# Sums of squares on another engine in the opening, paired first blocks in the short down stages, and head norms one block sooner, in a fused streaming encoder step

## The chip, the cores and the metric

One core of one Trainium2 chip runs the whole program. The engines are TensorE (PE; its weight loads are PEld), VectorE (DVE), ScalarE (ACT), GpSimd (POOL) and SyncE (SP), which issues the weight loads from HBM. The metric is the device time of one execution in microseconds. Before: a median of 2714.54 us over 3 runs, 2713.57 to 2715.55.

## The reference, cut

Two groups of requests (512 prompt tokens, 8 samples of 16 tokens, so 640 token columns) go through two layers of width 1024:

```python
def run_trunk(x, p, ...):
    for i in range(DEPTH):                                   # 2 layers
        x = x + 0.5 * swiglu(rmsnorm(x, norm_g[i, 0]), ffn_w_gu[i, 0], ffn_w_d[i, 0])
        xn = rmsnorm(x, norm_g[i, 1])
        y, st = even_mixer(xn, ...) if i % 2 == 0 else odd_mixer(xn, ...)
        x = x + y
        x = x + 0.5 * swiglu(rmsnorm(x, norm_g[i, 2]), ffn_w_gu[i, 1], ffn_w_d[i, 1])
        xg = rmsnorm(x, norm_g[i, 3])
        x = x + (p[i] @ w_ple[i]) * jax.nn.sigmoid(xg @ w_ple_gate[i])
    y = rmsnorm(x, final_norm)

def even_mixer(xn, ...):
    qkv_a, z_a, beta_a, a_a, q_b, k_b, v_b, o_b, i_b, f_b = split(xn @ w_in)
    qkv_a = silu(causal_dwconv(hist, gdn_conv_w))
    q_a = l2norm(q_a.reshape(B, T, H_A, DK_A)) * (DK_A ** -0.5)   # the head norms: 4 of q, 4 of k
    k_a = l2norm(k_a.reshape(B, T, H_A, DK_A))
    ...  # gated delta rule and mLSTM, chunked; output projection
```

The hidden width of each SwiGLU is 2816. All is computed in float32.

## The kernel before, in words

Activations lie transposed: `x` is 128 partitions by 8 blocks (KD) by 640 tokens. Every weight block (a 128-column strip, `kt` k steps of 128 rows) is split into a high part `whi` (ScalarE's cast, `prep`, L1595 to L1607) and a low part `wlo` (POOL's subtraction, L861, or DVE's in places), and every activation likewise (`xh`/`xl`, `hh`/`hl`). A product `mm` (L898 to L919) makes, in each k step, six matmuls of 128x320: high by high, high by low and low by high for both halves of the tokens. Results go to one of four PSUM slots; semaphore `job_done` tells of a finished block, `slot_free` of a free slot. The high and low parts of a block lie in a ring of three pairs of slots (`place_run` gives the order), so a cast waits until the block that had its slots is done. The order of work on each engine is written out by hand, stage by stage; each engine goes through its own list in order.

The opening (`kind == "load"`): PE transposes the eight blocks of x (L982) and, between them, makes the k steps of the first two weight blocks as the low parts `xl` come (`x_low`, L2269). ScalarE copies x (L1787), makes `xh` (L1650), and after its loop casts the third block (`prep(2)`) and squares the blocks of x (L1813). DVE copies the rest of x, makes `xl`, the tau sums (L2228 to L2231, `tau_sums`, inputs of the FFN's fast products), the copies of the states, and then adds the squares up (`square_sum`, L2278 and L2280). Behind the third block PE multiplies the sum by a matrix of ones (`norm_job`, L968), ScalarE takes the root (L1732), DVE the reciprocal (L2366). POOL makes the low parts from the third block on. `plain_start` is DVE's order in the first FFN stage.

Each FFN is done in three parts of 8, 8 and 6 hidden blocks (PARTS): a "gu" stage that makes them and a "down" stage that multiplies them by `kt` = 8, 8 or 6 k steps into the eight blocks of x. Block 0 of a down stage waits in each k step for the hidden block (`h_ready`, from `hidden_low`, L2793); with `kt` = 6 it is the last part (`last`), and for every finished block DVE scales it (L2181), updates x (L2919), adds the square that ScalarE makes (L1659, L2280) and makes the new low part (L2269), while ScalarE makes the high part (L1650) and casts the weight block after the next but one. In the second FFN of a layer (`"pT" in s`), PE transposes the layer's embedding behind block 1 and DVE copies it (L2941, L2943). The next stage's first block takes the x blocks k step by k step (`xg_ready`) and is followed by its norm product.

The even mixer's stage `even_in` has 12 convolved blocks (NA), a block of gates, and 12 plain blocks. DVE also makes the rows of the gates (`row_steps`, in the first five plain blocks). The head norms are tied to the plain blocks: from block HN_LAG = 4 on, ScalarE squares one head (L1739), PE sums it (L968), ScalarE takes the root (L1747, one tile `root`, so it waits for DVE's use of the root before), DVE the reciprocal and the scaling (`head_norm`, L2373, L2374). Then `core` starts: PE drains the slots, spreads rows (L1051), fills with blocks of z and waits for DVE's scaled keys (L2398) at L1057.

## Time and profile before

| what | us |
|---|---|
| median of 3 runs | 2714.54 |
| profiled execution, its own time | 2713.01 |
| its span, first to last instruction | 2711.3 |
| PE busy | 2652.8 |
| PEld busy | 2613.9 |
| DVE busy | 1863.9 |
| ACT busy | 1075.4 |
| POOL busy | 524.6 |

The mean granted clock of TensorE is 0.991 of full speed; it is below 1 in the opening, at some places between 866 and 959 us (the end of the mixer's core) and at the very end. A matmul's duration in a row (about 0.31 us) is not its cost: they are pipelined, and starts are about 0.147 us apart. "Idle before" in square brackets is the time in which the engine had nothing, and behind the arrow stands what released it.

### The profile page before, as it was taken

How to read it: one execution, taken by the hardware profiler on the slowest of the kernel's cores; microseconds unless marked ns; L12 is line 12 of the kernel's file. 1: busy time of each engine (PE TensorE's matmuls, PEld its weight loads, DVE VectorE, ACT ScalarE, POOL GpSimd, SP SyncE). 2: the span in 40 equal slices, each digit the busy share in tenths (PEclk: the TensorE clock that was granted, in tenths of full speed). 3: DMA queues.
4: the chain of work that ended last, by engine and by line, in shares of the span. 5: the costliest groups of instructions: out<-in, count | busy, mean ns of one | idle time of the engine just before them, and what ended most of it. 6: DMA issues, size and time to landing. Idle time of an engine off the chain costs nothing.

```text
span 2711.3 us, 43605 instructions
## 1 busy us (share of the span) xinstructions
PE 2652.8 (98%) x18155; PEld 2613.9 (96%) x18155; DVE 1863.9 (69%) x2188; ACT 1075.4 (40%) x1565; POOL 524.6 (19%) x249
## 2 busy tenths in 40 slices
PE   7999999999999999999999999999999999999998
PEld 7999999999998799999999999999999999999998
DVE  7748386988667768576577874847666786584756
ACT  5525254233222645344244552524411254252545
POOL 1030303232010030201113302030333311102041
PEclk9999999999999999999999999999999999999999
DMA  4323223232003122323232232232222223232231
GB/s 122 86 71 89 83 75 90 55 81 55 17 9 86 54 72 78 94 78 94 63 88 70 71 101 71 78 94 75 83 78 79 63 78 94 63 95 65 82 101 50
DMA packets 401180, 205.57 MB, mean 76 GB/s; under 512 B 15586, under 2 KB 398971, under 8 KB 400984
## 3 DMA queue, kind: packets, MB, share of 16 engines
q1 hardware_dynamic: 400778, 202.70, 26.4%
q8 instruction: 144, 2.36, 0.4%
q14 instruction: 52, 0.43, 0.1%
q10 hardware_dynamic: 206, 0.08, 0.0%
HBM read 195.14 MB, written 7.60 MB: 75 GB/s over the span
## 4 chain that ended last, share of the span: by engine, by line
PE 54%; DVE 9%; ACT 2%; issue 1%; POOL 0%; DVEq 0%; ACTq 0%
PE ps L928 9%; PE ps L930 9%; PE ps L929 9%; PE ps L913 9%; PE ps L917 8%; PE ps L914 8%; DVE ut L2181 1%; DVE x L2919 1%; DVE sumsq L2280 1%; DVE r L2366 1%; DVE hf L2787 1%; DVE x L3105 0%; DVE wlo L2197 0%; DVE hl L2269 0%; PE ps L1198 0%
## 5 line engine op out<-in xcount | busy, mean ns | idle before, releaser
L861 POOL TENSOR_TENSOR wlo<-raw,whi 128x1024 fp32r<-128x1024 f32 (+2 forms) x212 | 513.1, 2423 | 2147.0 <-ACT whi L1607 2146.6
L913 PE MATMUL ps<-xh,whi 128*128 128x320 f32 x1520 | 464.0, 313 | 12.1 <-POOL wlo L861 4.7
L914 PE MATMUL ps<-xl,whi 128*128 128x320 f32 x1520 | 458.4, 309 | 0.0
L913 PE MATMUL ps<-hh,whi 128*128 128x320 f32 x1440 | 437.6, 312 | 5.1 <-DVE hl L2793 2.9
L914 PE MATMUL ps<-hl,whi 128*128 128x320 f32 x1440 | 434.8, 310 | 0.0
L928 PE MATMUL ps<-tau_hi,whi 128*128 128x320 f32 x1296 | 401.3, 310 | 2.1 <-DVE wlo L2197 2.0
L929 PE MATMUL ps<-tau_lo,whi 128*128 128x320 f32 x1296 | 400.5, 309 | 0.0
L930 PE MATMUL ps<-tau_hi,wlo 128*128 128x320 f32 x1296 | 400.5, 309 | 0.0
L1607 ACT CAST whi<-raw 128x1024 fp32r<-128x1024 f32 (+2 forms) x214 | 206.7, 967 | 395.0 <-PE ps L917 355.6
L917 PE MATMUL ps<-xh,wlo 128*128 128x320 f32 x1520 | 347.1, 310 | 0.0
L917 PE MATMUL ps<-hh,wlo 128*128 128x320 f32 x1440 | 329.1, 310 | 0.0
L2181 DVE TENSOR_TENSOR ut<-ps,r 128x640 f32<-128x640 f32 x112 | 92.4, 825 | 328.0 <-PE ps L917 327.0
L913 PEld LDWEIGHTS ps<-xh,whi 128*128 128x128 f32 x1520 | 286.3, 188 | 18.5 <-issue 11.0
L914 PEld LDWEIGHTS ps<-xl,whi 128*128 128x128 f32 x1520 | 286.3, 188 | 0.9 <-issue 0.2
L1618 ACT CAST whi<-raw 128x512 fp32r<-128x512 f32 (+1 forms) x243 | 185.0, 766 | 246.9 <-PE ps L930 125.6
L913 PEld LDWEIGHTS ps<-hh,whi 128*128 128x128 f32 x1440 | 271.4, 189 | 8.1 <-DVE hl L2793 4.5
L914 PEld LDWEIGHTS ps<-hl,whi 128*128 128x128 f32 x1440 | 271.3, 188 | 0.4
L917 PEld LDWEIGHTS ps<-xh,wlo 128*128 128x128 f32 x1520 | 254.7, 188 | 0.0
L928 PEld LDWEIGHTS ps<-tau_hi,whi 128*128 128x128 f32 x1296 | 243.2, 188 | 4.5 <-issue 3.9
L929 PEld LDWEIGHTS ps<-tau_lo,whi 128*128 128x128 f32 x1296 | 243.3, 188 | 0.0
L930 PEld LDWEIGHTS ps<-tau_hi,wlo 128*128 128x128 f32 x1296 | 243.3, 188 | 0.0
L917 PEld LDWEIGHTS ps<-hh,wlo 128*128 128x128 f32 x1440 | 241.4, 188 | 0.0
(433 smaller groups left out, 4829.4 us busy)
## 6 DMA issues: line engine op xcount, KB each, us to landing
raw<-in_ffn_w_gu SPq DMA_DIRECT2D x324, 256.0 KB, 3.9
raw<-in_ffn_w_d SPq DMA_DIRECT2D x64, 512.0 KB, 4.0
raw<-in_w_in_even SPq DMA_DIRECT2D x32, 512.0 KB, 4.1
raw<-in_ffn_w_d SPq DMA_DIRECT2D x32, 384.0 KB, 3.6
raw<-in_w_in_odd SPq DMA_DIRECT2D x24, 512.0 KB, 3.7
raw<-in_w_ple_gate SPq DMA_DIRECT2D x16, 512.0 KB, 3.9
raw<-in_ffn_w_gu SPq DMA_DIRECT2D x14, 512.0 KB, 4.6
raw<-in_w_out_even SPq DMA_DIRECT2D x8, 512.0 KB, 4.0
```

The costliest lines, as they stand in the source:

```text
L861: pool.tensor_tensor(ring(wlo, n), raw[:, slot, 0:kt, :], ring(whi, n).bitcast(fp32), ALU.subtract).then_inc(lo_ready, 1)
L913: pe.matmul(ps[j % 4][:, c, 0:HT], wh[:, k], hi[:, k, cs], start=(k == 0), stop=False)
L914: pe.matmul(ps[j % 4][:, c, 0:HT], wh[:, k], lo[:, k, cs], start=False, stop=False)
L917: last = pe.matmul(ps[j % 4][:, c, 0:HT], wl[:, k], hi[:, k, cs], start=False, stop=(k == kt - 1))
L928: pe.matmul(out, whi[:, w], hi(i), start=(start and i == 0), stop=False, skip_group_check=True)
L929: pe.matmul(out, whi[:, w], lo(i), start=False, stop=False, skip_group_check=True)
L930: last = pe.matmul(out, wlo[:, w], hi(i), start=False, stop=(i == KH - 1), skip_group_check=True)
L1607: act.copy(ring(whi, n), raw[:, raw_pos["block", n], 0:kt, :]).then_inc(hi_ready, 1)
L1618: act.copy(group_ring(whi, g), group_raw(p, g)).then_inc(pair_hi, 1)
L2181: o1(dve.tensor_tensor(out, a, b, ALU.mult))
L2280: own(dve.tensor_tensor(sumsq[:], sumsq[:], src, ALU.add).then_inc(sm, 1), sm)
L2366: o1(dve.reciprocal(r[:], r[:]))
```

## The change

Three edits. (1) In the opening ScalarE's squares move into its loop over x, two blocks behind the high parts, the cast of the third weight block moves from behind the loop to its step 5, and the first two blocks' results are copied out after the squares. The additions of the squares go from DVE to POOL: `add_square(1)` to `add_square(3)`, then the third block's low part, then `add_square(4)` to `add_square(7)`. In `plain_start` the order of three steps changes. (2) In down stages with fewer than 8 k steps PE makes all steps but the last of blocks 0 and 1, then the last step of both. (3) HN_LAG goes from 4 to 3, so that the eight head norms go with plain blocks 3 to 10 in place of 4 to 11.

```diff
--- before.py
+++ after.py
@@ -457,7 +457,7 @@
         gcol0 = 4 * HA * P
         bcol = [gcol0 + 2 * HA + q * HB * P for q in range(4)]
         icol = bcol[3] + HB * P
-        HN_LAG = NA - 2 * HA
+        HN_LAG = NA - 2 * HA - 1
         s = dict(kind="even_in", n0=len(blocks), prod=prod - 1, pos=[], l2=[], side=side(prod - 1))
         for q in range(3):
             for h in range(HA):
@@ -472,7 +472,7 @@
                 blk((w_in, bcol[q] + h * P), KD, "plain")
                 s["pos"].append([8, 12, 20][q] + h)
 
-                if q * HB + h >= HN_LAG:
+                if HN_LAG <= q * HB + h < HN_LAG + 2 * HA:
                     s["l2"].append(job("hn"))
         stages.append(s)
         Z_ORDER = [0, 1, 2, 4, 3, 5, 6, 7]
@@ -861,9 +861,21 @@
                 pool.tensor_tensor(ring(wlo, n), raw[:, slot, 0:kt, :], ring(whi, n).bitcast(fp32),
                                    ALU.subtract).then_inc(lo_ready, 1)
 
-            n = 2
+            def add_square(q):
+
+                pool.wait_ge(sq_ready, q + 1)
+                a, b = ([qcopy, stt] if q == 1 else [sumsq, [qcopy, stt][q % 2]])
+                step(pool.tensor_tensor(sumsq[:], a[:], b[:], ALU.add))
+                pool.sem_inc(sq_added, 2 if q == 1 else 1)
 
             pool.wait_ge(lo_ready, 2)
+            for q in range(1, 4):
+                add_square(q)
+            low(2, KD)
+            for q in range(4, KD):
+                add_square(q)
+            pool.sem_inc(sumsq_done, 1)
+            n = 3
             while n < NB:
                 kt = blocks[n][1]
                 if n == 12:
@@ -1516,8 +1528,15 @@
                 elif kind == "down":
                     if s.get("split"):
                         first_blocks(s)
+                    hidden = (h_ready, s["hbase"])
+                    both = s["kt"] < KD
+                    if both:
+                        for part in ((0, s["kt"] - 1), (s["kt"] - 1, s["kt"])):
+                            for o in range(2):
+                                mm(s["n0"] + o, *s["hid"], first=hidden, part=part)
                     for o in range(2 if s.get("split") else 0, KD):
-                        mm(s["n0"] + o, *s["hid"], first=(h_ready, s["hbase"]) if o == 0 else None)
+                        if not both or o > 1:
+                            mm(s["n0"] + o, *s["hid"], first=hidden if o == 0 else None)
                         if o == 1 and "pT" in s:
 
                             pe.wait_ge(p_loaded, 32 * (s["layer"] + 1))
@@ -1536,7 +1555,7 @@
                         tposes(j, [((b - first) // 4, b % 4 * P, cacoll[:, b, :]) for b in range(first, last)])
                     for b in range(NA):
                         mm(n + NA + 1 + b, *s["side"])
-                        if b >= HN_LAG:
+                        if HN_LAG <= b < HN_LAG + 2 * HA:
                             q = b - HN_LAG
 
                             pe.wait_ge(hn_sq, s["hn0"] + q + 1)
@@ -1781,6 +1800,12 @@
                     act.dma_start(vstage[a:b, 1, :], ins["conv_c_w"][0].rearrange("j (k p) -> (j k) p", p=P)).then_inc(in_loaded[1], 16)
                     act.dma_start(vstage[b:b + HB, 1, :], ins["mlstm_norm_w"][0].rearrange("(k p) -> k p", p=P)).then_inc(in_loaded[1], 16)
                     act.dma_start(vstage[b + HB:b + HB + 1, 1, :], ins["gdn_norm_w"]).then_inc(in_loaded[1], 16)
+                    def square(q):
+                        if q >= 2:
+
+                            act.wait_ge(sq_added, q - 1)
+                        act.activation([qcopy, stt][q % 2][:], x[:, q, :], ACT.Square).then_inc(sq_ready, 1)
+
                     for q, j in enumerate(s["x"]):
 
                         act.wait_ge(job_done, done_at(j))
@@ -1798,7 +1823,10 @@
                         x_high(0, q, 0)
                         if q == 0:
                             prep(1)
-                    prep(2)
+                        if q >= 2:
+                            square(q - 2)
+                        if q == 5:
+                            prep(2)
 
                     def first_out(n, out):
                         j = block_job[n]
@@ -1806,16 +1834,11 @@
                         act.wait_ge(job_done, done_at(j))
                         act.copy(halves(out[:]), ps[j % 4][:, :, 0:HT]).then_inc(slot_free[j % 4], 1)
 
-                    for q in range(KD):
-                        if q >= 2:
-
-                            act.wait_ge(sq_added, q - 1)
-                        act.activation([qcopy, stt][q % 2][:], x[:, q, :], ACT.Square).then_inc(sq_ready, 1)
-                        if q == 3:
-                            first_out(0, gt)
-                            prep(3)
-                        if q == 5:
-                            first_out(1, ut)
+                    square(KD - 2)
+                    square(KD - 1)
+                    first_out(0, gt)
+                    prep(3)
+                    first_out(1, ut)
                 elif kind == "gu":
                     p0, count, n0 = s["p0"], s["count"], s["n0"]
 
@@ -1957,14 +1980,15 @@
                         own(act.activation(c, a, ACT.Relu, bias=bias, scale=sgn).then_inc(row_act, 1), row_act)
                     for b in range(NA):
                         q = b - HN_LAG
-                        if q >= 0:
+                        heads_due = 0 <= q < 2 * HA
+                        if heads_due:
                             if q == 0:
 
                                 act.wait_ge(conv_out, NA)
                             head_squares(s, q, s["l2"], qkv[:, q, :])
                         if b >= 2:
                             prep_next(n + NA + 1 + b, 2)
-                        if q >= 0:
+                        if heads_due:
                             head_root(s, q, s["l2"][q], 1.0)
                 elif kind == "core":
                     z0 = s["z0"]
@@ -2755,9 +2779,6 @@
                     o1(dve.tensor_copy(ccstate[:].rearrange("p a b -> p (a b)"), ps[j % 4][:, 1, 0:KD * DECB * CC]))
                     o1(dve.tensor_copy(vec2[:], ps[j % 4][:, 1, KD * DECB * CC:KD * DECB * CC + NV2]))
                     free(j)
-                    for q in range(KD):
-                        square_sum(0, q)
-                        dve.sem_inc(sq_added, 1)
                 elif kind == "gu":
                     p0, count = s["p0"], s["count"]
 
@@ -2831,12 +2852,12 @@
                     def plain_start():
                         t = s["tau"]
                         tau_rest(t, 0)
-                        tau_rest(t, 1)
                         norm_recip(s)
                         copied_gate()
-                        tau_sums_alone(3)
+                        tau_rest(t, 1)
                         copied_hidden()
                         plain_gate(1)
+                        tau_sums_alone(3)
                         tau_rest(t, 2)
                         hidden_low(0)
                         if s["plain"] > 3:
@@ -3065,7 +3086,7 @@
                         if b < len(row_steps):
                             row_steps[b]()
                         q = b - HN_LAG
-                        if q >= 0:
+                        if 0 <= q < 2 * HA:
                             head_norm(s, q, qkv[:, q, :], float(DK) ** -0.5 if q < HA else 1.0)
                 elif kind == "core":
```

## Rows read from the trace of the kernel before

**Rows 1.** The page, busy time (share of the span) and instructions of each engine.

```profile
PE 2652.8 (98%) x18155; PEld 2613.9 (96%) x18155; DVE 1863.9 (69%) x2188; ACT 1075.4 (40%) x1565; POOL 524.6 (19%) x249
```

**Rows 2.** PE's waits over the span: engine line <- releaser: total us, times, longest.

```profile
PE ps L968 <- DVE sumsq L2280: 5.1, 2, 4.9
...
PE ps L913 <- DVE hl L2793: 2.9, 6, 0.8
```

**Rows 3.** PE in order of time, opening: start, us, what, idle before <- releaser.

```profile
28.81 0.41 PE L913 MATMUL ps<-xh,whi 128*128 128x320 f32 x1 [0.67 <-DVE xl L2269]
...
34.03 0.31 PE L913 MATMUL ps<-xh,whi 128*128 128x320 f32 x1
...
46.09 2.50 PE L968 MATMUL ps<-sumsq,one 128*128 128x320 f32 x4 [4.87 <-DVE sumsq L2280]
```

**Rows 4.** Windows: PE, PEld, DVE, ACT, POOL busy (x), granted clock, DMA share, GB/s.

```profile
41.00:51.00 10.00, 5.13 (x17) 4.12 (x16) 8.19 (x7) 8.18 (x10) 4.18 (x2) 0.66 0.38 107
```

**Rows 5.** DVE in order of time, opening.

```profile
27.88 0.88 DVE L2269 SCALAR_TENSOR_TENSOR xl<-x,vec,xh 128x640 fp32r<-128x640 f32 x1
...
30.14 2.61 DVE L2228 SCALAR_TENSOR_TENSOR tau_row<-x,vec,xg_back 128x320 f32<-128x320 f32 x1
...
45.22 0.83 DVE L2280 TENSOR_TENSOR sumsq<-sumsq,stt 128x640 f32<-128x640 f32 x1
```

**Rows 6.** POOL in order of time, opening and first short down stage.

```profile
30.02 2.37 POOL L861 TENSOR_TENSOR wlo<-raw,whi 128x1024 fp32r<-128x1024 f32 x1 [25.35 <-ACT whi L1607]
...
424.65 1.84 POOL L861 TENSOR_TENSOR wlo<-raw,whi 128x768 fp32r<-128x768 f32 x1 [5.46 <-ACT whi L1607]
...
437.10 2.03 POOL L861 TENSOR_TENSOR wlo<-raw,whi 128x768 fp32r<-128x768 f32 x1 [2.98 <-ACT whi L1607]
442.11 2.04 POOL L861 TENSOR_TENSOR wlo<-raw,whi 128x768 fp32r<-128x768 f32 x1 [2.98 <-ACT whi L1607]
```

**Rows 7.** PE and DVE in order of time, layer 0, first FFN's last down stage.

```profile
424.82 0.42 PE L913 MATMUL ps<-hh,whi 128*128 128x320 f32 x1 [0.84 <-DVE hl L2793]
...
469.81 1.24 PE L968 MATMUL ps<-sumsq,one 128*128 128x320 f32 x4
...
426.08 0.82 DVE L2181 TENSOR_TENSOR ut<-ps,r 128x640 f32<-128x640 f32 x1 [1.31 <-PE ps L917]
...
443.43 1.39 DVE L2919 SCALAR_TENSOR_TENSOR x<-ut,x 128x640 f32<-128x640 f32 x1
...
467.80 0.89 DVE L2269 SCALAR_TENSOR_TENSOR xl<-x,vec,xh 128x640 fp32r<-128x640 f32 x1
```

**Rows 8.** ScalarE, DVE and PE in order of time, layer 0, second FFN.

```profile
1410.42 0.84 ACT L1607 CAST whi<-raw 128x768 fp32r<-128x768 f32 x1 [2.22 <-PE ps L917]
...
1410.43 0.82 DVE L2181 TENSOR_TENSOR ut<-ps,r 128x640 f32<-128x640 f32 x1 [1.31 <-PE ps L917]
1421.41 0.69 DVE L2941 CAST hh<-ps 128x512 fp32r<-128x512 f32 x1
...
1452.82 0.38 PE L913 MATMUL ps<-xh,whi 128*128 128x320 f32 x1 [0.32 <-issue]
```

**Rows 9.** PE and DVE in order of time, layer 1, second FFN.

```profile
2581.14 0.41 PE L913 MATMUL ps<-xh,whi 128*128 128x320 f32 x1 [1.52 <-DVE xl L2793]
...
2626.35 0.39 PE L913 MATMUL ps<-xh,whi 128*128 128x320 f32 x1 [0.73 <-POOL wlo L861]
...
2587.67 0.82 DVE L2181 TENSOR_TENSOR ut<-ps,r 128x640 f32<-128x640 f32 x1 [0.99 <-PE ps L917]
```

**Rows 10.** ScalarE, DVE and PE in order of time, head norms and the core's start.

```profile
609.69 0.80 ACT L1747 ACTIVATE root<-ps,eps 128x640 f32<-128x640 f32 x1 [9.24 <-DVE qkv L2374]
...
604.59 4.15 DVE L2373 RECIPROCAL inv<-root 128x640 f32<-128x640 f32 x1
...
612.79 1.24 PE L968 MATMUL ps<-sq,one 128*128 128x320 f32 x4
...
655.64 0.57 PE L1051 MATMUL ps<-R,ident 128*128 128x128 f32 x3 [1.09 <-issue]
...
662.98 1.16 PE L1057 MATMUL ps<-W,qkv 128*128 128x128 f32 x8 [1.70 <-DVE W L2398]
```

## The prediction

> **What bounds the kernel now.** The first look goes to the busy table: TensorE (PE) is busy for 98% of the span [rows 1]. So only time in which PE stands still, or runs at the lower clock, can be won; some 58 us in all. The second look is the list of PE's waits: the longest one by a compute engine is the single wait of 4.9 us for the opening's sum of squares; the one on the hidden blocks comes six times and adds up to 2.9 us [rows 2]. The third look, PE's order of time, places them. In the opening PE's third block begins at 34.03 and would go straight into the norm product, but this starts at 46.09 after 4.87 idle [rows 3]; the granted clock from 41 to 51 us is 0.66, so part of that stretch ran at 1.2 GHz in place of 2.4 [rows 4]. That block gives the unit for all below: eight k steps (six matmuls each) from 34.03 to 41.2, 0.88 us a step with the last one's drain.
>
> **The opening.** Removed: eight operations of DVE, the last of which ends at 46.05 [rows 5]. Added: seven additions of 128x640 on GpSimd (POOL), from about 19 us on, interleaved with DVE's own work, and the third block's low part between them. No row has such an addition. The nearest are POOL's subtractions: 1.84 us for 768 columns, 2.37 for 1024 [rows 6], so 2.07 ns a column and 1.58 us for 640. Upper bound 1.84; below 1.3 nothing speaks for. Seven are 11 us.
>
> What they lie beside decides. At 30.02 POOL starts its only subtraction of this stretch; DVE's 128x320 operation issued at 30.14 takes 2.61 us and ends 0.36 after POOL's, where the like are near 0.55 [rows 5, 6]. So a DVE operation with two SBUF inputs stands still while POOL reads SBUF, and here nearly all of DVE's are such. At 442.11 the reverse is seen: POOL takes 2.04 in place of 1.84 since DVE was in first [rows 6]. They take turns.
> The Trainium skill, SBUF — State Buffer, "SBUF: two separate sides", states the same as a rule: the pair of ports is an exclusive lock held for a whole instruction. By this rule the move from DVE to POOL buys no overlap in the opening; without it the opening would gain 6.5 us (rival A). The trace agrees with the rule in the operation at 30.14.
>
> Walking the order: addition 1 (19.1 to 20.7) holds up the low part of x block 3, PE loses 0.3. Addition 2 falls into the tau sums, so that x block 4's low part ends 2.3 us late, at 26.0. Addition 3, the third block's low part and addition 4 (1.6 + 2.4 + 1.6) all fall on the next four tau sums, which stand ahead of x block 6 on DVE. PE starts that step at 28.81 now, right behind DVE's operation of 27.88, after a wait of 0.67 [rows 3, 5]: no cover. It moves to about 35.5, with 5.4 us of idle PE before it. x block 7 and everything behind are ready (last addition near 42). From 35.5 PE has two steps, the state transposes (1.4) and the third block: 1.8 + 1.4 + 1.8 + 7.2 = 12.2, so the norm product starts at 47.7, against 46.09, and wants no wait. The new stall draws the lower clock as the old one did, which costs 0.8 to 2.5 after it; but the norm product (2.50 us now [rows 3], 1.24 at the full clock [rows 7]) and the block behind it lose the 2.6 us that they pay today. Net: +1.6 + 1.6 - 2.6 = **+0.6 us**. Bounds: -6.5 (no blocking) and +4 (POOL's operations keep the ports back to back). The new order behind it (tau low part 1 later, the last tau sums later) moves DVE by about 1 us under blocks that keep PE busy for 21 us: nothing.
>
> **The down stages with six k steps (four: layer 0 and 1, each FFN).** Now PE does five steps, waits for the sixth hidden block (0.84, 0.84, 0.84 and 1.52 idle), finishes block 0 and goes on. The change puts five steps of block 1 (4.4 us) into the wait. Face value: the whole loss, 1.0 + 1.0 + 1.0 + 1.7 = -4.7 us. What this moves: block 0 is finished after eleven steps in place of six and the wait: in the first case from 426.0 to 429.4, +3.4. Behind it hangs DVE's chain of each block (scale, update x, ScalarE's square, sum, low part), on which ScalarE's next cast and POOL's next low part hang too. Its period is 5.01 us [rows 6] (its last two starts), PE's is six steps, 5.28. So a late start is won back by 0.27 a block at most, and the last two periods of a stage are longer than PE's (bigger weights, next stage).
> First case: DVE starts block 0 at 426.08 and makes the last x low part from 467.80 on; PE needs it at its own 468.8 and starts the norm product at 469.81 [rows 7]. No cover. After: block 0's chain begins at 429.5, block 1's is not held up by the idle gap of today, and its update ends at 436.2 against 434.8; +1.4 stays to the end, the norm product starts **+1.3**. The third case (layer 1, first FFN) has the same ring order: **+1.3**.
> Second case (layer 0, second FFN): the weight ring gives block 2 the slots of block 0. ScalarE casts block 2 at 1410.42, the moment that block 0 is done, and DVE begins at 1410.43 [rows 8]. Both move by the whole 3.4. Here DVE also copies two transposed blocks (4.3 us), so its chain runs without idle to the end of the stage, and PE's gate block of the next stage waits for it (0.32 idle at 1452.82 [rows 8], a cast behind that chain): **+3.4**.
> Fourth case: block 0 is done 2.7 later (the stall is longer today), the chain's idle wait for block 1, which starts at 2587.67 [rows 9], takes some back; the rest reaches the small blocks that PE waits for at 2626.35 [rows 9]: **+2.3**.
> Sum **+8.3 us**; bounds -4.7 (face value) and +13.6 (3.4 in each). I take the sum since in each case a row shows PE at zero slack on that chain.
>
> **Head norms a block sooner.** Gain: after the last block no norm follows. PE waits 1.09 before 655.64 and 1.70 before 662.98 [rows 10], the latter for a product that stands behind a reciprocal and a scaling of DVE (5.0 us). Without these it is ready by 660.2 and PE, from 655.4 on 5.4 us of work, is there at 660.9: -2.1. Cost: the four first norms move into DVE's and ScalarE's crowded time. The root of head 1 waits 9.24 us for DVE's head 0, whose reciprocal starts at 604.59 [rows 10], behind the row steps. Now head 2's sum at 612.79 just finds its square; with the shift the fourth sum stands there (613.5), whose square waits for root 2, which waits for DVE's head 1: 609.2 + 5.0 = 614.3, then root and square 1.7: 616.0. PE stalls 2.4 (0.8 if POOL misses DVE's row steps). Net **+0.3**, bounds -2.1 and +0.8.
>
> **Sum.** 0.6 + 8.3 + 0.3 = +9.2 on the profiled execution's 2713.0 gives 2722.2; the median shown is 1.5 above that execution: 2723.8. Five new stalls of 2 to 5 us lie between ones that left the clock (1.70) and one that took it down (4.87); one more episode at 1.2 GHz, priced by half the lost 2.6, is 0.7 on average where DVE's pace doesn't hide it: **2724.5 us**.
>
> **Rivals.** A: POOL and DVE work side by side in the opening. For it: both only read most of those tiles. Against: the 2.61. Opening -6.5, in all +2.1: 2716.6. Chance 0.13.
> B, the other side: DVE's later start is absorbed and the down stages give their face value. It decides by whether the last x low part is later than PE's seventh step into the next stage; today's distance is 0.1 us. With opening +0.6 and heads -1: -5.1, 2709.4; with A as well -13, 2701. Together 0.12.
> C: the new stalls bring the lower clock several times, unhidden: +15 to +18, 2729.5 to 2732.5. Chance 0.13.
> D: the reordered blocks don't change PE's waits at all, since DVE's chain hides it: within 2 of 2714.5. Chance 0.04. The forecast, 2718 to 2729: 0.58.
>
> Range 2712 to 2730. 0.2% is 5.4 us, about what a measurement of this kernel can tell from none. Faster than 2709.1: 0.09. Slower than 2720: 0.69 (forecast 0.55, C 0.13, a little of A). Same: 0.22.
>
> **What would show it.** Right: DVE operations of 2 us and more between 19 and 42 us, and PE idle over 4 us ahead of x block 6; no wait before the opening's norm product; PE waiting for an x low part just ahead of the norm product behind both first FFNs; in the second FFNs PE waiting 2 to 3 us for POOL at down block 5; a wait of 2.4 for a head's square near 614. Wrong: PE entering the third block before 36 us; the norm product of the even mixer starting earlier relative to its down stage than now; 2716 or less.

## The result and the profile after

| kernel | median us | lowest to highest | runs | ratio to before (95%) |
|---|---|---|---|---|
| before, beside it | 2714.06 | 2709.13 to 2721.57 | 6 | |
| after | 2732.4 | 2724.65 to 2734.18 | 6 | 1.0065 (1.0051 to 1.0079) |

Slower by 0.65%, 2.4 us above the range (2712 to 2730). The ratios here and below are not the quotients of the medians and differ from them by up to 0.1%. One execution of the kernel before, of those beside e5 to e8, took 3698.81 us at a mean clock of 0.651 and is left out of the ratios. The profiled execution took 2734.18 us, its span 2732.4 at a mean granted clock of 0.986 (before: 2711.3 at 0.991). The executions of the changed kernel fall into two groups of spans, near 2723 and near 2731; the profiled one is of the upper. Where the gap of 8 us between them is made is asked below. The kernel before has groups too: of its 88 other executions on record 23 have spans of 2705.6 to 2707.8, 3 of 2709.3 to 2709.9, 59 of 2711.2 to 2714.2 and 3 of 2719.8 to 2720.9; the trace of before is of the third.

The busy table of after, to set against [rows 1]. DVE's eight additions are gone (2188 to 2180 instructions), POOL has seven more, and PE, whose work is the same, is busy for 15.5 us more, though it has the same 18155 matmuls: the first sign that the granted clock is part of the answer.

```profile
PE 2668.3 (98%) x18155; PEld 2627.5 (96%) x18155; DVE 1866.6 (68%) x2180; ACT 1074.1 (39%) x1565; POOL 535.4 (20%) x256
```

PE's waits of after, in the form of [rows 2]. The wait of 4.9 for the sum of squares is gone from the list. In its place stand the low part of x (`xl`) in the opening, POOL's low parts (`wlo`) in the down stages and the head's square (`ut`).

```profile
PE ps L925 <- POOL wlo L861: 11.0, 15, 2.7
PE ps L925 <- DVE xl L2293: 9.1, 4, 3.5
...
PE ps L980 <- ACT ut L1758: 2.3, 1, 2.3
...
PE ps L925 <- DVE hl L2293: 1.6, 1, 1.6
```

POOL in order of time in the opening of after (L868 is the addition, L861 the third block's low part):

```profile
19.29 1.58 POOL L868 TENSOR_TENSOR sumsq<-qcopy,stt 128x640 f32<-128x640 f32 x1 [14.63 <-ACT stt L1807]
...
27.06 2.10 POOL L868 TENSOR_TENSOR sumsq<-sumsq,stt 128x640 f32<-128x640 f32 x1 [3.49 <-ACT stt L1807]
29.34 2.42 POOL L861 TENSOR_TENSOR wlo<-raw,whi 128x1024 fp32r<-128x1024 f32 x1 [0.18 <-POOL sumsq L868]
31.73 1.78 POOL L868 TENSOR_TENSOR sumsq<-sumsq,qcopy 128x640 f32<-128x640 f32 x1
```

DVE beside it. The tau sums take 0.55 where POOL is idle and 1.7 to 2.6 where it is not; each ends 0.3 to 0.4 after the POOL operation beside it.

```profile
27.79 1.73 DVE L2252 SCALAR_TENSOR_TENSOR tau_row<-x,vec,xg_back 128x320 f32<-128x320 f32 x1
29.55 2.57 DVE L2253 SCALAR_TENSOR_TENSOR tau_row<-x,vec,xg_back 128x320 f32<-128x320 f32 x1
32.16 1.70 DVE L2254 SCALAR_TENSOR_TENSOR tau_row<-x,vneg,tau_row 128x320 f32<-128x320 f32 x1
33.89 0.55 DVE L2255 SCALAR_TENSOR_TENSOR tau_row<-x,vneg,tau_row 128x320 f32<-128x320 f32 x1
```

And PE in order of time, with every new wait of the three edits and the norm product of the opening, which waits for nothing, to set against [rows 3], [rows 7] to [rows 10]:

```profile
26.27 0.48 PE L925 MATMUL ps<-xh,whi 128*128 128x320 f32 x1 [2.09 <-DVE xl L2293]
...
35.61 0.41 PE L925 MATMUL ps<-xh,whi 128*128 128x320 f32 x1 [3.47 <-DVE xl L2293]
...
50.80 0.70 PE L980 MATMUL ps<-sumsq,one 128*128 128x320 f32 x2
...
472.41 0.41 PE L925 MATMUL ps<-xh,whi 128*128 128x320 f32 x1 [1.53 <-DVE xl L2293]
...
619.91 0.54 PE L980 MATMUL ps<-ut,one 128*128 128x320 f32 x1 [2.35 <-ACT ut L1758]
...
663.52 0.68 PE L1063 MATMUL ps<-R,ident 128*128 128x128 f32 x4 [1.21 <-issue]
...
1430.73 0.38 PE L925 MATMUL ps<-hh,whi 128*128 128x320 f32 x1 [0.99 <-POOL wlo L861]
1449.47 0.39 PE L925 MATMUL ps<-hh,whi 128*128 128x320 f32 x1 [2.67 <-POOL wlo L861]
...
1983.17 0.41 PE L925 MATMUL ps<-hh,whi 128*128 128x320 f32 x1 [1.55 <-DVE hl L2293]
...
2624.39 0.61 PE L925 MATMUL ps<-xh,whi 128*128 128x320 f32 x1 [2.64 <-POOL wlo L861]
2647.88 0.39 PE L925 MATMUL ps<-xh,whi 128*128 128x320 f32 x1 [0.77 <-POOL wlo L861]
```

The traces are compared by landmarks that PE passes once: the norm products (their start), the core's first matmul, the core's last transpose; and one of DVE, the last hidden block's low part in the first FFN. Each entry is the difference of that landmark's time to the first trace of before, less the same at the landmark ahead of it. In brackets stands the time at the lower clock in that stage. "Whole" is the changed kernel; the second to fourth column of it are further executions of the same program (e4, e13, e14), and e11 is the kernel before once more.

| stage, up to | before | after | whole, e4 | whole, e13 | whole, e14 | before, e11 |
|---|---|---|---|---|---|---|
| norm product of the opening | 46.09 (5.6) | +4.7 (10.2) | +5.5 (17.1) | +1.7 (6.8) | +4.9 (13.7) | +1.4 (1.2) |
| last hidden block of FFN 1 | 423.94 (4.7) | -2.1 (0) | -2.1 (0) | -2.1 (0) | -2.1 (0) | +0.5 (5.6) |
| norm of even mixer | 469.81 (0) | +1.0 (0) | +1.0 (0) | +1.0 (0) | +1.0 (0) | 0 (0) |
| core's start | 655.64 (0) | +4.3 (3.4) | +4.3 (3.4) | +4.2 (3.4) | +2.7 (0) | 0 (0) |
| core's end | 959.72 (30.7) | +6.4 (47.8) | -1.6 (30.7) | -0.1 (34.1) | -1.8 (30.7) | +8.4 (47.8) |
| norm behind FFN 2, layer 0 | 1459.93 (0) | +4.2 (3.4) | +3.0 (0) | +4.2 (3.4) | +3.0 (0) | -0.1 (0) |
| norm of odd mixer | 1964.73 (0) | +0.9 (0) | +0.9 (0) | +0.9 (0) | +0.9 (0) | 0 (0) |
| norm behind FFN 2, layer 1 | 2643.48 (0) | +2.1 (3.4) | +2.1 (0) | +2.1 (3.4) | +2.1 (0) | 0 (0) |
| end | 2711.28 (8.4) | -0.4 (6.0) | 0 (7.3) | -0.3 (6.1) | 0 (7.2) | -0.4 (5.4) |
| sum | | +21.2 | +13.1 | +11.5 | +10.5 | +9.7 |

Two things are read from it. What the edits do comes again from execution to execution, but for the opening (+1.7 to +5.5) and for 1.2 to 1.6 us in two stages where 3.4 us at the lower clock come or stay away: +10.5 to +13.1 in all where the core runs about as in the first trace. And the largest single entry of after, +6.4 in the core, is one that the unchanged kernel has too, in e11.

### The profile page after: what moved, and what is told of

Read it like the earlier page. It is cut to its first block, busy times and chain, and to the rows that moved or that the text cites. A ratio compares the mean times of both kernels' runs of the same rounds, so it can differ in the third digit from the quotient of the medians.

```text
span 2732.4 us, 43606 instructions
## 1 busy us (share of the span) xinstructions
PE 2668.3 (98%) x18155; PEld 2627.5 (96%) x18155; DVE 1866.6 (68%) x2180; ACT 1074.1 (39%) x1565; POOL 535.4 (20%) x256
## 3 DMA queue, kind: packets, MB, share of 16 engines
q1 hardware_dynamic: 400778, 202.70, 26.2%
## 4 chain that ended last, share of the span: by engine, by line
PE 79%; DVE 16%; ACT 2%; issue 2%; POOL 0%; DMA 0%; DVEq 0%; SPq 0%; ACTq 0%
PE ps L940 12%; PE ps L941 12%; PE ps L942 12%; PE ps L925 11%; PE ps L929 11%; PE ps L926 11%; PE ps L1069 3%; DVE x L2940 2%; PE ps L1095 2%; DVE ut L2205 1%; DVE sumsq L2304 1%; DVE ct L2995 1%; PE ps L1063 1%; DVE ct L2992 1%; DVE r L2390 1%
## 5 line engine op out<-in xcount | busy, mean ns | idle before, releaser
L861 POOL TENSOR_TENSOR wlo<-raw,whi 128x1024 fp32r<-128x1024 f32 (+2 forms) x212 | 511.6, 2416 | 2135.8 <-ACT whi L1626 2135.4
L925 PEld LDWEIGHTS ps<-hh,whi 128*128 128x128 f32 x1440 | 271.5, 189 | 11.5 <-issue 5.9
```

Source lines behind the costliest of these rows:

```text
L861: pool.tensor_tensor(ring(wlo, n), raw[:, slot, 0:kt, :], ring(whi, n).bitcast(fp32), ALU.subtract).then_inc(lo_ready, 1)
L925: pe.matmul(ps[j % 4][:, c, 0:HT], wh[:, k], hi[:, k, cs], start=(k == 0), stop=False)
```

## The experiments

**One edit alone (e1 to e3), and all three again (e4).** The theory was three separate mechanisms: the shared ports in the opening, DVE's chain in the short down stages, the row steps ahead of the head norms. The rival for each was that its part does nothing or gains.

e1, the opening alone (cut and put in fewer lines; the new order in `plain_start` is in it too):

```diff
@@ POOL
+            for q in range(1, 4): add_square(q)
+            low(2, KD)
+            for q in range(4, KD): add_square(q)
@@ ScalarE, loop over x
+                        if q >= 2: square(q - 2)
+                        if q == 5: prep(2)
@@ DVE
-                    for q in range(KD): square_sum(0, q) ...
```

> The opening's edit alone. The theory (GpSimd's additions and VectorE's work take turns on SBUF, so the x block steps of TensorE are held up ahead of a stall of some 3.5 us): the norm product of the opening starts near 50.8 us as in the changed kernel, every later stage is shifted by 2.5 us and no more, time +2.5 us against the kernel before. Rival (the reordered start of the first FFN or the clock behind it costs on its own): a shift that grows behind 60 us. Rival that the core's lower clock belongs to this edit: +10 us.

Measured: 2716.72 us (11 runs) beside 2713.49, ratio 1.0013 (1.0005 to 1.0022), so +3.2 us; its trace is of its fastest execution (2713.78) and shows +0.8. PE waits 5.00 ahead of x block 6, and the norm product comes at 48.72, where 50.8 was expected: +2.6, with 2.1 of it given back behind it:

```profile
35.00 0.64 PE L925 MATMUL ps<-xh,whi 128*128 128x320 f32 x1 [5.00 <-DVE xl L2285]
```

e2, the down stages alone:

```diff
+                    both = s["kt"] < KD
+                        for part in ((0, s["kt"] - 1), (s["kt"] - 1, s["kt"])):
+                            for o in range(2): mm(s["n0"] + o, *s["hid"], first=hidden, part=part)
```

> The paired first blocks alone, in the four down stages with six k steps. The theory (TensorE has no slack on VectorE's chain, which starts 3.4 us later): +1.0, +4, +1.0 and +2.5 us at the four stages, +8.5 us in all. Rival (the later start of VectorE's chain is absorbed, face value): -4.7 us. The waits for the sixth hidden block, 0.84 us thrice and 1.52 once, are gone in either case.

Measured: 2720.9 us (6 runs), ratio 1.0033 (1.0021 to 1.0045), so +7.4 us. By stages, counted from the last hidden block: +1.2, +4.3 (with 3.4 us at the lower clock), +1.1, +2.1.

e3, the head norms alone (the guards that end the eight heads at block 10 are cut here):

```diff
-        HN_LAG = NA - 2 * HA
+        HN_LAG = NA - 2 * HA - 1
```

> The head norms one block sooner, alone. The theory: TensorE waits 2.4 us for the square of the fourth head near 614 us, which also brings 3.4 us at the lower clock (1.7 lost), and gains 2.1 at the core's start: +2.0 us up to the core. Rival (the lower clock that cost 8 us in the core of the changed kernel comes with this edit, which makes the core start on another footing): +10 us in most runs. Without that: +2 us.

Measured: 2716.95 us (11 runs), ratio 1.0011 (1.0001 to 1.002), so +3.5 us, over executions that fall apart: spans of 2709.0 to 2709.3 (4 of 11), one of 2712.7 (the trace) and 2715.1 to 2717.5 (6 of 11). The wait came, and behind it 3.4 us at the lower clock: the stage ahead of the core is 4.2 us longer. In the core the gain stands in every trace of this edit: from the core's first matmul to the product at L1057 PE takes 5.49 us in place of 7.34, and from 10 to 140 us into the core it is 2.0 us ahead of before (in the whole change 1.7 from there on).

```profile
617.64 1.34 PE L968 MATMUL ps<-ut,one 128*128 128x320 f32 x4 [2.35 <-ACT ut L1739]
```

e4, the whole change:

> The changed kernel itself once more, beside the three parts and on the same chip. If the 8 us in the core are a matter of how the stretches at the lower clock fall in a run, the runs fall into two groups near 2723 and 2732 us, and runs of the kernel before show such groups too; if they belong to the change, all runs of the kernel before stay below 2716 and nearly all of this one lie near 2732.

Measured: 2728.67 us (6 runs), ratio 1.0062 (1.005 to 1.0075), so +15.2 us against 3.2 + 7.4 + 3.5 = 14.1 for the parts. The parts add up within 1.1, though that is in part luck, since the three slowest of the six executions of e4 belong to the upper group and the median lies between the groups. Stage by stage each edit's cost is found again in the whole. The opening and the down stages lose by their medians (3.2 and 7.4) as by their stages (0.5 in e1's fastest execution, and 8.7); of the heads the stages show a loss of 0.7 or 2.2 us, and the median's 3.5 holds more of the clock in the core than of the edit.

**How much of block 1 goes into the wait (e5).** If the later end of block 0 is what costs, one step of block 1 (0.88 us, as long as the wait) fills the wait and leaves block 0 where it was.

```diff
+                        last_ = s["kt"] - 1
+                        for o, part in ((0, (0, last_)), (1, (0, 1)), (0, (last_, s["kt"])), (1, (1, s["kt"]))):
+                            mm(s["n0"] + o, *s["hid"], first=hidden, part=part)
```

> Against the kernel before, in the four short down stages only one k step of block 1 (0.88 us) goes into TensorE's wait, so block 0 is finished when it is now. The theory (the stage ends by VectorE's chain, which begins with block 0): the wait's 3.5 us are worth nothing at stages one to three (0 to -0.2 us each) and at most 0.8 at the fourth, where the wait is longest; in all -1 us. Rival (TensorE itself is the bound, the paired kernel lost by something else): nearly the whole of the wait, -3.5 to -4.5 us.

Measured: 2716.66 us (11 runs), ratio 1.0009 (1.0 to 1.0018). The three waits of 0.84 are gone, and the fourth is 0.65 in place of 1.52:

```profile
2588.49 0.42 PE L913 MATMUL ps<-xh,whi 128*128 128x320 f32 x1 [0.65 <-DVE xl L2800]
```

The four down terms fall from +1.2, +4.3, +1.1, +2.1 to -0.9, -0.1, -0.9 and -0.4. So the loss was the later end of block 0. The expectation held in the sum's direction and missed in the first FFNs: there 0.9 of 1.0 is won where 0 to 0.2 was expected, so DVE's chain follows PE in these stages and doesn't bound them by itself. In the second case 0.1 of 1.0 reaches the norm product, as expected of a chain that is the bound. In the fourth, 0.87 less of the first wait is set against a wait for POOL that grows from 0.73 to 1.19. The sum is -2.2, for -1 expected; the median is 3.2 above before's. The trace puts this down to the core (+7.7, 47.8 us at the lower clock); 6 of the 11 executions, the profiled one among them, lie in an upper group of spans (2714.9 to 2718.1, the others 2710.3 to 2711.2), and that the five others of it have the same long core is not shown.

**The row steps later (e6).** If the heads' wait comes from row steps that stand ahead of head 1's reciprocal on DVE, two of them two blocks later take it away and leave the gain.

```diff
+                    ROW_AT = [0, 1, 2, 4, 6]
-                        if b < len(row_steps):
-                            row_steps[b]()
+                        if b in ROW_AT:
+                            row_steps[ROW_AT.index(b)]()
```

> Head norms one block sooner as in the change, but the last two row steps of VectorE (maxima, keys) wait for blocks 4 and 6 in place of 3 and 4, so that the first head norms stand ahead of them. The theory (the 2.4 us wait near 614 comes from VectorE's row steps ahead of head 1): no wait for a head's square, no stretch at the lower clock before the core, TensorE 2.1 us earlier at the core's first product than in the kernel before; 5 to 6 us faster than the heads' edit alone. Rival (the single tile of the roots is the cause whatever stands ahead): the wait stays, +3.5 us.

Measured: 2708.69 us (11 runs), ratio 0.9988 (0.998 to 0.9997). PE has no wait at a norm product from 600 us to 650, and DVE's two reciprocals stand 6.0 us apart:

```profile
603.93 4.15 DVE L2374 RECIPROCAL inv<-root 128x640 f32<-128x640 f32 x1
...
609.95 4.15 DVE L2374 RECIPROCAL inv<-root 128x640 f32<-128x640 f32 x1
```

In after the row steps lie between them (11.2 us from 601.93 to 613.11). With e3 it shows both sides of the third edit: a gain of 2.0, and a wait of 2.35 that is not part of it. Of the 4.4 us that the trace of e6 wins, 3.6 lie in the core; the 1.6 of them above the edit's 2.0 go with the clock there, 27.3 us at the lower one against 30.7.

**The additions taken away or halved (e7, e8).** The opening's edit again, with POOL's additions for q > 1 left out (e7) or over half of the columns (e8). The semaphores, the order and ScalarE's squares stay. In both the sum of squares lacks columns or blocks, so what is computed behind it is not the reference's.

```diff
@@ e7
-                step(pool.tensor_tensor(sumsq[:], a[:], b[:], ALU.add))
+                if q == 1:
+                    step(pool.tensor_tensor(sumsq[:], a[:], b[:], ALU.add))
@@ e8
-                step(pool.tensor_tensor(sumsq[:], a[:], b[:], ALU.add))
+                z = slice(0, T if q == 1 else HT)
+                step(pool.tensor_tensor(sumsq[:, z], a[:, z], b[:, z], ALU.add))
```

> The opening's edit with six of the seven additions on GpSimd left out (the sum of squares holds two blocks only, so the first norm is wrong); orders, waits and semaphores stay. The theory (GpSimd's additions hold VectorE's operations up): without them only the third block's low part holds VectorE, TensorE's waits of 2.1 and 3.5 us shrink to under 1 us together, the norm product starts near 42.5 us and the time is 5 to 7 us below the opening's edit. Rival (the waits come from ScalarE's new order, squares and cast in its loop): waits and norm product within 1 us of the opening's edit.

> The opening's edit with the six later additions on GpSimd over 320 columns in place of 640 (the rest of the sum is left out). GpSimd's 1.58 us become 0.9. The theory: each VectorE operation that an addition holds up ends 0.7 us sooner, so the step of x block 4 starts 0.7 and that of x block 6 some 2 us sooner than with the opening's edit (26.3 and 35.6 us), the norm product about 2 us sooner besides what the clock adds. Rival (ScalarE's order): no change at either step.

Measured: 2711.53 us (10 runs), 0.9993 (0.9984 to 1.0003), and 2712.81 us (10 runs), 0.9999 (0.999 to 1.0008). The wait ahead of x block 6 is 5.00 with the additions whole (e1), 3.66 with halves and 2.70 without. DVE's same tau sum (the third of x blocks 4 and 5) in e1, e8 and e7:

```profile
31.54 1.70 DVE L2246 SCALAR_TENSOR_TENSOR tau_row<-x,vneg,tau_row 128x320 f32<-128x320 f32 x1
```

```profile
30.57 1.03 DVE L2247 SCALAR_TENSOR_TENSOR tau_row<-x,vneg,tau_row 128x320 f32<-128x320 f32 x1
```

```profile
28.39 0.55 DVE L2247 SCALAR_TENSOR_TENSOR tau_row<-x,vneg,tau_row 128x320 f32<-128x320 f32 x1
```

The duration of DVE's operation follows that of POOL's (1.77, 1.11, none). The step of x block 6 starts at 33.35 with halves (33.6 expected) and at 30.70 without. The 2.70 that stay are not the additions': POOL's low part falls into the same tau sums, since ScalarE's cast of the third block was put into its loop. The rows of e7:

```profile
25.40 2.61 POOL L861 TENSOR_TENSOR wlo<-raw,whi 128x1024 fp32r<-128x1024 f32 x1 [5.94 <-ACT whi L1620]
...
25.77 2.58 DVE L2246 SCALAR_TENSOR_TENSOR tau_row<-x,vec,xg_back 128x320 f32<-128x320 f32 x1
```

So 2.3 of the 5.0 us are the additions, and of the rest the row of 2.58, where the like take 0.55, accounts for 2.0. That it is there because of the earlier cast is read from the rows; no run takes the cast alone back. The expectation for e7 fell short here: the waits at x blocks 4 and 6 were to shrink under 1 us together and are 0.90 and 2.70, and the norm product starts at 45.88, not near 42.5. Part of that is what the rival named, ScalarE's new order.

**An opening without POOL's additions (e9).** If the ports are the trouble and the norm's wait of 4.9 is DVE's additions coming late, the additions must stay on DVE, but start early: squares 0 to 3 in ScalarE's loop, first addition behind x low part 1, and the fourth block's low part behind them on DVE.

```diff
@@ ScalarE, loop over x
+                        if q == 2:
+                            square(0); square(1)
+                        if q in (3, 4):
+                            square(q - 1)
@@ DVE
+                        if q == 1:
+                            add_square(1)
...
+                    for q in range(2, KD):
+                        add_square(q)
+                    dve.wait_ge(lo_ready, 3)
+                    low(3)
```

> Another opening on the kernel before: the additions stay on VectorE, but the first lies in its idle time near 16 us, ScalarE squares blocks 2 and 3 in its loop and does its copies and the cast of the fourth weight block ahead of the other squares, and the fourth block's low part goes from GpSimd to VectorE behind the additions. The theory (the opening's wait is made of a chain of squares, additions and one of GpSimd's operations in it; VectorE's work ahead of it must not be held up): no wait at x block 4 or 6 beyond today's 0.7, the norm product starts near 42 us in place of 46, no stretch at the lower clock behind it, -5 us (4 to 7). Rival (the first FFN's start, VectorE's chain behind the norm, takes the gain back): -1 us or less.

Measured: 2709.11 us (12 runs), ratio 0.9992 (0.9982 to 1.0001). The norm product starts at 41.01 in place of 46.09, with hardly a wait:

```profile
28.34 0.41 PE L918 MATMUL ps<-xh,whi 128*128 128x320 f32 x1 [0.67 <-DVE xl L2280]
41.01 1.34 PE L973 MATMUL ps<-sumsq,one 128*128 128x320 f32 x4 [0.25 <-DVE sumsq L2748]
```

In the trace this is -5.7 to the end. The medians show 4.3, the ratio 2.2 with an interval that just touches 1: the groups of executions blur it (spans of 2703.4 to 2703.6 in 3 of 12, 2705.6 to 2714.2 in the rest).

**The three together (e10)**: e9, e6 and the one step of e5.

> The three mended edits together: the other opening, one k step of block 1 in the wait of the short down stages, head norms one block sooner with the later row steps. The theory (the parts add up, apart from how the lower clock falls in the core): -5 for the opening, -2 for the down stages, -3 for the heads, -10 us, 2703 to 2706 against the kernel before. Rival (what one part gives, a later stage takes back): less than -6 us.

Measured: 2709.96 us (12 runs), ratio 0.998 (0.9968 to 0.9992), the trace -6.6. It is faster than both kernels, but by 3.4 us by the medians and 5.4 by the ratio, where 10 were expected and under 6 was the rival's. In the traces the parts promise about twice what it shows; most of the difference is in the core, -0.5 with 34.1 us at the lower clock against -3.6 with 27.3 in e6. Its spans again fall apart, 2698.4 to 2698.9 (4 of 12) and 2704.7 to 2711.1.

**The kernel before, twice more (e11, e12).** Is the core's long stretch at the lower clock a thing of the change?

> The kernel before again, one look. Its runs fall into two groups, spans near 2707 and 2712 us with a granted clock of 0.993 and 0.991. The theory (the groups are the core's time at the lower clock, by how its stretches fall on the core's gaps): all stages outside the opening and the core are equal to the first trace within 0.5 us, and the core takes 304.1 us where it has 30.7 us at the lower clock, less with less. Rival: the difference lies in another stage, such as a weight load that came late.

> The kernel before a third time, as the look before it: core and opening may differ with the time at the lower clock, by about half of it, and nothing else may.

Measured: 2722.66 us for e11 and 2713.42 for e12. e12 repeats the first trace within 0.4 us; e11 has a core that is 8.4 us longer. All of it is made late: up to 206 us into the core the two traces differ by at most 0.03 us, and the stretches at the lower clock begin 211 us into it. Windows of 98 us up to the core's end, of before, of e11 and, 103 long, of after (start:end, length, then busy time and instructions of PE, PEld, DVE, ACT and POOL, granted clock, DMA share, GB/s):

```profile
862.00:960.00 98.00, 90.86 (x573) 77.44 (x571) 70.14 (x102) 46.41 (x103) 2.36 (x1) 0.84 0.35 92
```

```profile
863.00:961.00 98.00, 91.16 (x539) 76.80 (x537) 66.43 (x98) 46.60 (x103) 2.36 (x1) 0.79 0.36 92
```

```profile
871.00:974.00 103.00, 96.83 (x553) 82.38 (x554) 68.69 (x99) 43.83 (x96) 2.36 (x1) 0.77 0.31 83
```

PE is busy for nearly the same time in the first two, idle for 7.1 and 6.8 us, and gets 573 matmuls done in one and 539 in the other. The unchanged kernel does this too, so it is not by itself the edits' work.

**Where the groups of spans are made (e13 to e16).** The theory: in the core. The rival: by the new stalls. e13 and e14 are the changed kernel, e15 is e3, e16 is e2.

> The whole change once more, one profiled look. Two groups of spans are known: 2722.8 to 2724.4 and 2729.4 to 2732.4. Theory (the groups are made in the core of the mixer, by how long it runs at the lower clock): a span of the first group comes with some 27 to 34 us at the lower clock there and a core stage of about 302 us, one of the second with 44 to 51 us and about 310. Rival (the groups are made by the new stalls, in the opening and the down stages): the core stays at about 31 us in both, and the stages with stalls differ by 7 us.

> As the run before it: the core's time at the lower clock tells the group of the span (theory), or the stages with new stalls do (rival).

> The head norms' edit alone once more. Its spans lay at 2709.0 to 2709.3 and at 2715.1 to 2717.5, with 2712.7 in the trace. Theory (core's clock): the stage ahead of the core is +4.2 again, with 3.4 us at the lower clock, and what differs from the first trace is the core's: 302 us with 31 us at the lower clock, 0.5 us more or less for each us of it. Rival: the wait for the head's square comes with other lengths, 1 to 8 us.

> The down stages' edit alone once more. The sizes of its four terms in the first trace were +0.9, +4.3, +1.1 and +2.1, the second with 3.4 us at the lower clock. If the stalls' lengths are fixed by the order of DVE's work, the same four come again within 0.3, but for the second, which is +4.3 with the lower clock and about +3.0 without it.

Measured: 2724.53, 2723.52, 2710.91 and 2720.16 us. Both executions of the changed kernel fell into the lower group, with 34.1 and 30.7 us at the lower clock in the core, where the one of the upper group (after) has 47.8. e15 has the least of all, 20.5 us, and the shortest core. (Its stage ahead of the core was expected at +4.2 again; it is +2.7, without time at the lower clock.)

```profile
860.00:958.00 98.00, 90.92 (x609) 77.89 (x608) 74.01 (x109) 46.88 (x104) 2.35 (x1) 0.90 0.40 103
```

All traces lie near one line. Against before, with the 2.0 of the heads' edit taken out where it is in: 20.5 us at the lower clock give -3.8, 27.3 give -0.9 to -1.6, 30.7 give -0.1 to +0.7, 34.1 give +1.6 and +1.9, 47.8 give +7.7 to +8.4. Above 30.7 us that is about half of the difference in time at the lower clock, below it a third to a half. The stages outside the core sum to +14.7 us in after, which is of the upper group, and to +14.7 (e4), +11.6 (e13) and +12.4 (e14) in the three traces of the lower group. So e4 and after differ in sum by the core alone: 8.0 us of span, 8.0 us of core. The 8 us between the groups are made there, as far as one trace of the upper group can tell. e16 repeats the four down terms of e2: +1.2, +4.3, +1.1, +2.1.

Not settled: why the upper group is common in the changed kernel (7 of 14 executions) and in e5 (6 of 11), and rare in the kernel before, where three executions with a span above 2719 stand against 85 below 2715. It is not bound to one edit: e3 and e10 have such a group (6 of 11 and 8 of 12), and so has e5, which leaves the heads alone, while the seven executions of e2 and e16 lie within 2 us. The edits don't touch the core's work. Something in when it starts or what ran ahead of it may choose, and no run here isolates that.

## Why the prediction was right or wrong

**The bound: right.** The loss is PE's time alone: new waits, and time at 1.2 GHz.

**The opening: the steps right, the clock under-sized.** The additions take 1.58 where DVE leaves the ports alone, which is the length worked out from POOL's subtractions [rows 6]. x block 4's low part ends at 26.2 (forecast 26.0). x block 6's step starts at 35.61 (forecast 35.5). The 5.4 of idle time were forecast in one piece ahead of that step; it came as 2.09 ahead of x block 4 and 3.47 ahead of x block 6, 5.6 in all, since the late low part of block 4 has no cover on PE either. The norm product waits for nothing and starts at 47.74 in e13, forecast 47.7, but at 50.8 to 51.6 in the three other traces. There more of the time behind the first of the two stalls was at the lower clock: 10.2 to 13.7 us, against 3.4. I had let the clock cost 0.8 to 2.5 behind the start, to be set off against the 2.6 of today. What was set off came right (the norm product takes 1.24 again, and the stage behind gives back 2.1 in every trace); what was paid was up to 3.9 more. Counted at the last hidden block of the first FFN, the term is -0.5 (e13), +0.5 (e1), +2.6 (after), +2.8 (e14) and +3.4 (e4), for a forecast of +0.6. But traces with the opening of before differ there by as much, from -0.6 (e2) to +1.9 (e11), so one trace cannot size this term to better than 2 us. Over all traces the five with this opening lie at +1.8 on average and the nine with the old one at +0.6: 1.2 us apart. Rival A is out: e7 and e8 show that the duration of DVE's operation goes with that of POOL's. (Its sum with B, given as -13 and 2701, should read -12.2 and 2702.3.)

**The down stages: right in sum, and in mechanism but for one reading.** Forecast +1.3, +3.4, +1.3, +2.3, in all +8.3. Measured in e2 +1.2, +4.3, +1.1, +2.1, in all +8.7, the second +3.0 where the lower clock didn't follow (e4, e14). The face value of -4.7 (rival B) is out. PE waits where the forecast said: 1.53 and 1.55 for the last x low parts ahead of the norm product behind the first FFNs (in layer 1 the tile is called `hl`, the two sets change places; L2293 is the same line), 2.67 and 2.64 for POOL at down block 5 in the second ones. The late start of DVE's chain, in after and by the last hidden block's low part, which is 2.6 late itself:

```profile
426.52 0.83 DVE L2814 TENSOR_TENSOR hl<-hf,hh 128x640 fp32r<-128x640 f32 x1 [0.86 <-ACT hh L1858]
431.95 0.82 DVE L2205 TENSOR_TENSOR ut<-ps,r 128x640 f32<-128x640 f32 x1 [4.60 <-PE ps L929]
```

The chain starts 5.4 behind the hidden block, in before 2.1 (426.08 [rows 7] from 423.94): 3.3 later, forecast 3.4. The reading that was wrong is "no cover" in the first FFNs: e5 starts their norm product 0.9 sooner with block 0 where it was. DVE's chain had that much to give once PE was sooner; what made it the bound in the changed kernel was its late start.

**The heads: both terms right, their echo missed.** The wait is 2.35 (forecast 2.4), the gain 2.0 (forecast 2.1). What was missed: the short wait drew 3.4 us at 1.2 GHz behind it in four of six traces with this edit (after, e3, e4, e13: +4.2 in the stage; e14, e15: +2.7). So the term is +0.7 or +2.2, for +0.3.

**The clock: the step that failed.** The prediction charged 0.7 us for time at 1.2 GHz behind all new stalls together, and nothing for the core, whose time at 1.2 GHz it took from one trace as if it were fixed. Both were too little: in after they are 2.8 us behind the stalls and 8.4 in the core. The 0.7 was one episode among five stalls, because 1.70 had left the clock alone and 4.87 had not. Stalls of 2.35 to 2.67 were followed by an episode, a stretch of 3.4 us at the lower clock, in eleven of eighteen cases: at the heads in four of six, at the second FFN of layer 0 in four of six (after, e2, e13, e16; not e4, e14), and at that of layer 1 in three of six (after, e13, e16). In layer 1 the stage is as long with it as without (+2.1), since DVE's pace hides it, as the prediction allowed. Two windows of after, the first at the lower clock and the second behind it, show what an episode does: in equal time 15 matmuls run in one and 25 in the other.

```profile
1449.83:1453.24 3.41, 3.41 (x15) 3.41 (x14) 2.47 (x4) 2.18 (x3) 0.94 (x1) 0.50 0.14 38
1453.24:1456.65 3.41, 3.41 (x25) 3.41 (x24) 2.39 (x3) 1.61 (x3) 1.08 (x1) 1.00 0.30 74
```

The two that cost something cost 1.2 and 1.6 us each, 2.8 together in after, and the opening 2.0 over the forecast. With these, after without the core's 8.4 is at +12.7 for a forecast of +9.9, which would still lie inside the range. This much of rival C was right, though not its +15 to +18: that the measured 2732.4 lies in its range is luck, as it takes the core's 8.4 us, which e11 has without any new stall; the clock behind the new stalls gave 4.8 at most.

**The core: the term put at nothing.** The rest is the upper group. Its 8.4 us, in half of the changed kernel's 14 executions and in four of these six, decide the median: 2732.4. The prediction took one trace of before as the kernel's state. e11, a trace of the same kernel, has a core 8.4 us longer, and no term and no bound of the sum allowed for that. What makes the long core more frequent in the changed kernel stays open.

## What to carry to other kernels

Before work is moved to POOL, look in the trace for one operation of DVE that ran beside one of POOL's: if it is as long as POOL's, the two took turns there, and additions that are moved will delay whatever stands behind DVE. A wait is worth filling only as far as the block that it ends stays where it was: fill it with as much as it is long (e5), not with all that is ready (e2). Price a new stall of PE of 2.4 to 2.7 us, in work that keeps PE full, as itself plus the 1.2 to 1.6 us that the lower clock cost behind more than half of those here; take more than one trace of a stage in which the clock falls, and compare stages, not totals, before an edit is blamed for what a stage does that it doesn't touch.

## What was not expected of the hardware

The same program's core ran with 30.7 us at the lower clock in two executions and 47.8 in a third (e11, e12 and the first trace), and the core was 8.4 us longer with it, though nothing of the program differed; over all kernels, whose code for this stage is the same, it was 20.5 to 47.8. The idle time of PE hardly differs (7.1 and 6.8 us in the windows above); the clock does (0.84 and 0.79).

A POOL addition of 128x640 took 1.58 where DVE left it alone, and up to 2.10 in DVE's company: the two take turns operation by operation. DVE's, when it came second, ended 0.35 or 0.36 after POOL's; POOL's was longer by 0.22, 0.52, 0.20 and 0.32 where DVE's had 0.37, 0.69, 0.39 and 0.49 left. The Trainium skill, SBUF — State Buffer, "SBUF: two separate sides", has the lock that the prediction weighed: the one that starts first has the ports for its whole instruction; the four rows of DVE above (1.73, 2.57, 1.70, 0.55) agree with it.
